# Layers, merge outputs and MLP down tiles: the high weights times both token halves as one 512-column matmul, and the two sums added at eviction

## The reference, cut to what matters

```
# first block, twice
h = rms_norm(x, norm_g);  p = h @ w_in                # fox, diff, moba: q, k, v, gate; gla: q, k, v, gate; a few small columns
fox  = forgetting_attention(q, k, v, log_f) * silu(gate)
diff = rms_norm((softmax(q1 k1) - lam * softmax(q2 k2)) v) * (1 - lambda_init) * silu(gate)   # q, k rotated
moba = moba_attention(rotated q, rotated k, v) * silu(gate)                                  # one block of 256: causal
gla  = rms_norm(gla_chunked(q, k, v, log_a)) * silu(gate)
x = x + concat(fox, diff, moba, gla) @ w_out
# second block, once
p, pc = modulate(norm(x)) @ in_w, modulate(norm(ctx)) @ in_w[:, :A_COLS + B_COLS]
ya, yb = rwkv7_branch(...), gdn_branch(...)           # recurrences over the context, then over the tokens, in both directions
x = x + g1 * ((gate_a * (ya @ up_a) + gate_b * (yb @ up_b)) @ out_w)
x = x + g2 * (square(relu(modulate(norm(x)) @ mlp_w1)) @ mlp_w2)
out = rms_norm(x)
```

## Time and profile before

| | |
|---|---|
| median of three runs | 3850.47 us (3849.56, 3850.47, 3851.57) |
| profiled execution | 3848.72 us, span 3846.6 us |
| mean granted clock of TensorE | 0.984 |
| busy, share of the span | PE 96%, PEld 89%, DVE 54%, POOL 43%, ACT 39% |
| DMA | 153 GB/s in the mean |

### The profile page before, as it was taken

The page is one execution under the profiler, slowest core; times in us unless marked ns, Lnnn a source line. Parts: engine busy times, 40 slices in busy tenths (PEclk is TensorE's granted clock), DMA queues, the critical chain, the costliest instruction groups (busy, mean ns, idle before and its releaser), DMA issues. The chain is left out here.

```text
span 3846.6 us, 85962 instructions
## 1 busy us (share of the span) xinstructions
PE 3682.1 (96%) x37216; PEld 3409.0 (89%) x37216; DVE 2084.0 (54%) x3808; ACT 1504.8 (39%) x2641; POOL 1659.3 (43%) x1195
## 2 busy tenths in 40 slices
PE   7999999999998999999899999999988999999998
PEld 7999898999986888888688888888888999999998
DVE  5545425444336776677766666666547553435343
ACT  5344434444434432322233333333334453435353
POOL 5555556555544543333311111111115566666664
PEclk9999999999989999999999999999999999999999
DMA  6445454454445777778410000100007445455553
GB/s 238 169 180 181 187 196 156 167 185 176 175 154 175 259 261 266 250 258 293 154 32 20 15 24 28 28 20 15 3 2 263 176 176 187 177 186 184 179 186 131
DMA packets 116391, 587.20 MB, mean 153 GB/s; under 512 B 20912, under 2 KB 40496, under 8 KB 51376
## 3 DMA queue, kind: packets, MB, share of 16 engines
q1 hardware_dynamic: 116016, 581.71, 42.5%
HBM read 560.95 MB, written 20.71 MB: 151 GB/s over the span
## 5 line engine op out<-in xcount | busy, mean ns | idle before, releaser
L557 PE MATMUL bank<-act_L,part_L 128*128 128x256 f32 x7296 | 946.6, 288 | 12.4 <-DMA cst<-in_cst 4.6
L557 PEld LDWEIGHTS bank<-act_L,part_L 128*128 128x128 f32 x7296 | 901.0, 193 | 49.1 <-issue 30.6
L557 PE MATMUL bank<-act_P,part_P 128*128 128x512 f32 (+1 forms) x3488 | 716.1, 365 | 17.9 <-POOL part_P L3013 12.8
L3013 POOL TENSOR_TENSOR part_L<-wring,part_L 128x512 fp32r<-128x512 f32 x304 | 532.8, 1754 | 458.0 <-ACT part_L L1325 449.7
L3013 POOL TENSOR_TENSOR part_C<-wring,part_C 128x512 fp32r<-128x512 f32 x320 | 567.6, 1782 | 370.1 <-ACT part_C L1325 370.1
L557 PEld LDWEIGHTS bank<-act_P,part_P 128*128 128x128 f32 x3488 | 590.4, 188 | 136.9 <-DVE arena_P L2437 16.0
L557 PE MATMUL bank<-arena_B 64*64 64x64 f32 (+2 forms) x11200 | 544.4, 231 | 39.2 <-DVE arena_B L2550 21.0
L557 PEld LDWEIGHTS bank<-arena_B 64*64 64x64 f32 (+2 forms) x11200 | 481.3, 143 | 89.2 <-DVE arena_B L2550 23.4
L3013 POOL TENSOR_TENSOR part_P<-wring,part_P 128x512 fp32r<-128x512 f32 x184 | 306.1, 1669 | 428.1 <-ACT part_P L1325 428.1
L1325 ACT ACTIVATE part_C<-wring 128x1024 fp32r<-128x1024 f32 x320 | 338.4, 1058 | 355.8 <-PE bank L557 352.7
L557 PE MATMUL bank<-act_Y,part_C 128*128 128x258 f32 (+1 forms) x3840 | 463.7, 283 | 9.5 <-POOL part_C L3013 9.5
(11 more groups left out here) (250 smaller groups left out, 3483.0 us busy)
## 6 DMA issues: line engine op xcount, KB each, us to landing
wring<-in_w SPq DMA_DIRECT2D x404, 1024.0 KB, 4.8
arena_P<-in_w SPq DMA_DIRECT2D x64, 1024.0 KB, 5.2
mring<-in_w SPq DMA_DIRECT2D x32, 1024.0 KB, 6.6
z_kept<-arena_P SPq DMA_DIRECT2D x34, 256.0 KB, 5.6
z_kept<-arena_P SPq DMA_DIRECT2D x58, 128.0 KB, 5.4
xT<-z_kept SPq DMA_DIRECT2D x26, 256.0 KB, 2.8
arena_C<-z_kept SPq DMA_DIRECT2D x32, 128.0 KB, 3.4
cst<-z_kept SPq DMA_DIRECT2D x24, 128.0 KB, 2.1
```

Source lines behind the costliest of these rows:

```text
L557: return e.matmul(out, lhsT, rhs, start=start, stop=stop)
L3013: e.tensor_tensor(wl[:, 4:8, :], wring[s % NS][:, 8 * j + 4:8 * j + 8, :], wh[:, 4:8, :].bitcast(F32), sub).then_inc(*mark("pool_lo", "lop ...
```

## The change

1. `project`: where X is 256 tokens wide and the tile isn't one of the merge's `apart`, Wh by Xh and Wh by Xl become one matmul of 512 columns into both halves of the bank, as in P. Wl by Xh goes to the first half as before. `b[:, 0:256]` then holds Wh Xh + Wl Xh, `b[:, 256:512]` holds Wh Xl. This takes in all 76 tiles of both layers, the 16 merge outputs and the 64 MLP down tiles.
2. `rest` (transposes or rotation into the upper half of the bank before) is called after k = 5 and not k = 3.
3. Input tiles: ScalarE copies the upper half, scaled, to where the sum is to be; then VectorE adds the lower half to it, and that releases the bank or `raw`. The gates have four instructions: ScalarE copy, VectorE sum (frees the bank), in the next tile's place for `rest` ScalarE tanh into `L.rope`, VectorE (tanh + 1) times the sum.
4. Output tiles, merge outputs, MLP down: a second VectorE instruction adds the upper half to xT and frees the bank.
5. The small products of the gates at tiles 1 and 2 now stand ahead of those tiles' evictions.

```diff
@@ project (TensorE)
+                    wide = X.shape[-1] == 256 and not apart
...
-                        mm(o, wh[:, k, :], x[:, 0, :], first and k == 0, False)
-                        mm(o, wh[:, k, :], x[:, 1, :], False, False)
+                        if wide:
+                            mm(b.rearrange("p (s t) -> p s t", s=2), wh[:, k, :], x, first and k == 0, False)
+                        else:
+                            mm(o, wh[:, k, :], x[:, 0, :], first and k == 0, False)
+                            mm(o, wh[:, k, :], x[:, 1, :], False, False)
                         t = mm(o, wl[:, k, :], x[:, 0, :], False, end and k == 7)
+                        if k == 5 and j == 0 and rest is not None:
+                            rest()
                         if k == 3:
-                            if j == 0 and rest is not None:
-                                rest()
@@ evac (ScalarE), input tiles
-                        cp(L.raw[n % 3], ps, SCALE.get(kind, 1.0)).then_inc(*mark("act_layer", "raw", l, n))
...
-                        af(L.mix[:, m, :], ps, ACT.Tanh, scale=0.5).then_inc(*mark("act_layer", "gate", l, n))
+                    cp(dst, b[:, 256:512], SCALE.get(kind, 1.0)).then_inc(*mark("act_layer", "low", l, n))
@@ rest (ScalarE), gates
+                        w.wait_ge(done("sum", l, n))
+                        af(L.rope, L.mix[:, gate_of(n), :], ACT.Tanh, scale=0.5).then_inc(*mark("act_layer", "gate", l, n))
@@ evac (VectorE), input tiles
+                    w.wait_ge(done("low", l, n))
+                    if what == "g":
+                        mx = L.mix[:, gate_of(n), :]
+                        tt(mx, b[:, 0:256], mx, add).then_inc(*mark("dve_layer", "free", "pj", u))
...
+                    elif what == "v" or g in ("diff", "moba"):
+                        r = L.raw[n % 3]
+                        stt(r, b[:, 0:256], scale, r, mult, add).then_inc(*mark("dve_layer", "raw", l, n))
+                    else:
...
+                        stt(dst, b[:, 0:256], scale, dst, mult, add).then_inc(*mark("dve_layer", "free", "pj", u))
@@ rest (VectorE), gates
+                        stt(L.mix[:, m, :], L.rope, 1.0, L.mix[:, m, :], add, mult).then_inc(*mark("dve_layer", "gated", l, m))
@@ output tiles, VectorE (merge outputs and MLP down alike, with stt)
-                        tt(xT[:, c, :], xT[:, c, :], b[:, 0:256], add).then_inc(*mark("dve_x", "free", "pj", u))
+                        tt(xT[:, c, :], xT[:, c, :], b[:, 0:256], add).then_inc(*mark("dve_x"))
+                        own("dve_x")
+                        tt(xT[:, c, :], xT[:, c, :], b[:, 256:512], add).then_inc(*mark("dve_x", "free", "pj", u))
```

More of the change, by code:

```diff
@@ L496, in raw_before, with gate_of @@
             return ("rest" if LTILES[m][0][-1] == "v" else "rawfree", l, m)
+        def gate_of(n):
+            kind, h = LTILES[n]
+            return 12 + h if kind == "gg" else 4 * GROUPS.index(kind[:-1]) + h
         def mark(sem, *event):
@@ L1458, in f @@
                         w.wait_ge(done("th", l, 15))
-                        cp(L.raw[n % 3], ps, SCALE.get(kind, 1.0)).then_inc(*mark("act_layer", "raw", l, n))
+                        dst = L.raw[n % 3]
+                    elif g == "g" and what in "qk":
+                        dst = (L.gq if what == "q" else L.gk)[:, h, :]
                     elif what in "qk":
[L1461 to L1467, removed]
-                    else:
-                        m = 12 + h if g == "g" else 4 * GROUPS.index(g) + h
-                        af(L.mix[:, m, :], ps, ACT.Tanh, scale=0.5).then_inc(*mark("act_layer", "gate", l, n))
+                        dst = (L.q if what == "q" else L.k)[i % 2]
+                        w.wait_ge(done("score", l, i - 2, 0)) if i >= 2 else None
+                    else:
+                        dst = L.mix[:, gate_of(n), :]
+                    cp(dst, b[:, 256:512], SCALE.get(kind, 1.0)).then_inc(*mark("act_layer", "low", l, n))
                 return f
@@ L1476, in layer_in @@
                     yield from project("L", 76 * l + n, evac(l, n), beside)
+                    if n == 59:
+                        rest(l, n)()
                     if n == 0:
@@ L2159, in rest, with f @@
                 g, what = kind[:-1], kind[-1]
+                if what == "g":
+                    def f():
+                        m = gate_of(n)
+                        w.wait_ge(done("gate", l, n))
+                        own("dve_layer")
+                        stt(L.mix[:, m, :], L.rope, 1.0, L.mix[:, m, :], add, mult).then_inc(*mark("dve_layer", "gated", l, m))
+                    return f
                 if not (what in "qk" and g in ("diff", "moba")):
@@ L2179, in evac @@
                 g, what = kind[:-1], kind[-1]
-                if what != "g":
-                    return None
-                m = 12 + h if g == "g" else 4 * GROUPS.index(g) + h
+                i = (n - 12) // 4
                 def f(b, u):
[L2185 to L2188, removed]
+                    scale = SCALE.get(kind, 1.0)
+                    w.wait_ge(done("low", l, n))
+                    if what == "g":
+                        mx = L.mix[:, gate_of(n), :]
+                        tt(mx, b[:, 0:256], mx, add).then_inc(*mark("dve_layer", "free", "pj", u))
+                        counts.at[("sum", l, n)] = counts.last("dve_layer")
+                    elif what == "v" or g in ("diff", "moba"):
+                        r = L.raw[n % 3]
+                        stt(r, b[:, 0:256], scale, r, mult, add).then_inc(*mark("dve_layer", "raw", l, n))
+                    else:
+                        if g == "g":
+                            dst, name = (L.gq if what == "q" else L.gk)[:, h, :], (kind, l, h)
+                        else:
+                            dst, name = (L.q if what == "q" else L.k)[i % 2], (what, l, i)
+                        stt(dst, b[:, 0:256], scale, dst, mult, add).then_inc(*mark("dve_layer", "free", "pj", u))
+                        counts.at[name] = counts.last("dve_layer")
                 return f
@@ L2193, in layer_in, with ev @@
                 for n in range(60):
-                    ev = {1: lambda b, u: gates_in(l, at), 2: lambda b, u: gates_out(l)}.get(n, evac(l, n))
+                    def ev(b, u, n=n):
+                        if n == 1:
+                            gates_in(l, at)
+                        elif n == 2:
+                            gates_out(l)
+                        evac(l, n)(b, u)
                     yield from project("L", 76 * l + n, ev, rest(l, n - 1) if n else None)
+                    if n == 59:
+                        rest(l, n)()
                     if n == 0:
@@ L2916, in ev @@
                         w.wait_ge(done("g1h"))
-                        stt(xT[:, c, :], b[:, 0:256], K.g1h[:, c:c + 1], xT[:, c, :], mult, add).then_inc(*mark("dve_x", "free", "pj", u))
+                        stt(xT[:, c, :], b[:, 0:256], K.g1h[:, c:c + 1], xT[:, c, :], mult, add).then_inc(*mark("dve_x"))
+                        own("dve_x")
+                        stt(xT[:, c, :], b[:, 256:512], K.g1h[:, c:c + 1], xT[:, c, :], mult, add).then_inc(*mark("dve_x", "free", "pj", u))
                         counts.at[("x", 3, c)] = counts.last("dve_x")
@@ L2974, in ev @@
                         own("dve_x")
-                        stt(xT[:, c, :], b[:, 0:256], mod[:, 80 + c, 0:1], xT[:, c, :], mult, add).then_inc(*mark("dve_x", "free", "pj", u))
+                        stt(xT[:, c, :], b[:, 0:256], mod[:, 80 + c, 0:1], xT[:, c, :], mult, add).then_inc(*mark("dve_x"))
+                        own("dve_x")
+                        stt(xT[:, c, :], b[:, 256:512], mod[:, 80 + c, 0:1], xT[:, c, :], mult, add).then_inc(*mark("dve_x", "free", "pj", u))
                         counts.at[("x", 4, c)] = counts.last("dve_x")
```

5 lines of the change are left out of this document (4 added, 1 removed).

## The result

The changed kernel takes 3832.63 us in the median of five runs (3830.91 to 3834.19), the kernel before 3851.20 beside it. The ratio is 0.995, with a 95% interval of 0.9939 to 0.9961: 18.6 us faster, or 15 to 23 by the interval. The prediction was 3820 in a range of 3802 to 3838. The time is in the range and the direction is right, but the gain is 60% of the 30.7 us forecast, and the time lies 1.6 us above the likeliest case's own range (3806 to 3831). What was mis-sized is the subject of the rest.

A forecast was written before the change was run, and what follows sets the result against it. TensorE's queue was taken as the bound, plus short waits in the layers. Terms: -37.8 + 1.5 + 1.7 + 0.9 + 3 = -30.7 us, from 3848.72 to 3818.0; with medians 1.75 higher, 3820 us, range 3802 to 3838.

The forecast's parts named there:

- likeliest case: The forecast itself for the whole kernel: gain 20 to 45 us, own range 3806 to 3831, chance 0.69.
- the gain's mechanism: TensorE, wide tiles: each matmul costs 0.013 us over its columns, whichever its width; 3712 matmuls go.
- overhead goes with columns: Rival on TensorE's matmuls: 512-column step 0.240 us, pair 0.360, no gain, 7 us of waits stay; 3857, chance 0.05.
- VectorE's queue: Rival: VectorE stops at all 120 input tiles until ScalarE has copied, delaying queued work; 37 us slower, 3888, chance 0.05.
- The signs: Timeline checks: merge and MLP 9 to 17 us shorter, layers 10 to 27; layers far under twice the rest means waits.
- The pace: Wide tiles on TensorE: a 512- plus 256-column pair takes 0.3466 or 0.353 us, not 0.360; middle gain 37.8 us.
- The two bounds: TensorE's gain from the removed matmuls: 49.7 us at 0.3466 us a pair, 26.0 us at 0.353.
- Item 3: Start of the GLA part in each layer: tile 4's sum is queued ahead on busy VectorE; 0.9 us charged.
- Item 2: Last head of each layer: copy, sum, tanh and product now come before the mask; 1.7 us charged.
- Item 1: Ends of both layers and the MLP: one more add before the square that TensorE waits for; 1.5 us charged.
- Item 4: Some 20 places where TensorE already waits for fixed chains: faster tiles find them later; 3 us, bounds 0 and 8.
- What hides the rest: Added evictions at merge outputs, MLP down, layer outputs, steady input tiles and gates: covered by slack, cost 0.

The follow-up runs named there:

- e9_queue: Changed kernel with only tile 4's sum moved ahead of four GLA instructions in VectorE's queue: 3823.61 us, against 3831.68 for the changed kernel run again.
- e4_rest3: Changed kernel with rest (transposes and rotation) called after k = 3 of the first half and not k = 5: 3838.82 us.
- e5_tiles4_59: Changed kernel with tiles 4 and 59 of each layer (first value tile, last gate) narrow and evicted as before: 3825.00 us, against 3853.21 before the change.
- e12_best: Changed kernel with tile 4's sum earlier in VectorE's queue, odd k's matmuls turned (also P's 256-token tiles), tile 59 narrow: 3816.62 us.
- e1_halves: Changed kernel with the 512-column matmul taken apart into two of 256, new evictions kept: 3865.05 us, against 3850.79 before the change.
- e3_order: Changed kernel with the two matmuls of every odd k swapped in wide tiles: 3825.33 us, 7.3 less than the changed kernel.
- e7_rest7: Changed kernel with rest (transposes and rotation) called after k = 7 of the first half and not k = 5: 3834.99 us.
- e11_queue_order: Changed kernel with tile 4's sum earlier in VectorE's queue and odd k's matmuls turned in wide tiles and P's 256-token tiles: 3816.97 us.

## Why the prediction was right in its sign and short in its size

- **What bounds it, and the gain's mechanism: right.** TensorE's queue is the bound, a step costs 0.013 us over its columns, and 3712 matmuls fewer gave time. The rivals "overhead goes with columns" and "VectorE's queue" over the whole of the layers fell. The signs came out as put: 10.1 us less in the layers and 8.8 in merge outputs and MLP, far from twice as much, so waits took part of the gain.
- **The pace: the mechanism right, the size off.** 37.8 us was the middle of 26.0 and 49.7; 32.4 was measured by the medians, 30.2 by the stretches that the edit touches. The merge outputs and the MLP are nearly all slow (8.8 us, by 80 x 16 pairs x 0.007 = 9.0), the layers mixed (21.4). The two bounds held. That the middle is near is luck: it was a choice for want of a reason, and what picks the pace isn't known now either. The range's lower end, 3802, is below what its own terms give (3850.5 - 49.7 + 4 = 3804.8). The guess that the contiguous X might help was wrong where it could be seen alone, in the MLP.
- **Item 3, the GLA starts: the step that failed most.** I put 0.9 us, with "the sum of tile 4 is queued ahead". It is queued behind the GLA work: 69.46 and not 65.0. The half tiles around it (the two of tile 5 and the first of tile 6) are 4.1 and 3.9 us longer than before in the two layers, and e9_queue gave 8.1 back. The earlier trace rows showed a busy VectorE from 64.17 on; what I didn't do was to place the new instruction in the program's order among those rows. The rival on VectorE's queue was the same mechanism, spread over the input tiles where at k = 5 it acts in the first value tile of each layer, and at k = 3 in a few heads as well (e4_rest3).
- **Item 2, the last heads: right.** Mask 458.84 - 456.93 = 1.91 us after ScalarE's copy, 1.8 foretold, 0.95 before; the waits are 8.7 us against 6.8, 1.9 more and 1.7 foretold, and 6.8 again with tile 59 narrow (e5_tiles4_59, e12_best).
- **Item 1, the three ends: right as far as seen.** e1_halves has the half tiles after the first layer's end 0.7 us longer than before, where 0.5 was charged.
- **Item 4, existing short waits, 3 us: the size about right, the reason in part wrong.** The sixteen half tiles of the heads in which the changed kernel didn't get faster with the others, or got slower, come to 2.7 us. But in e1_halves, where no tile runs faster, the heads are 1.2 us longer than before all the same (0.5 and 0.7 in the table), in half tiles that are mostly the same ones. So nearly half of it belongs to the evictions and the place of rest, and not to tiles that run faster.
- **What hides the rest: nearly right.** Merge outputs, MLP and layer outputs: no cost seen. Input tiles at k = 5: the 1.2 us just named, besides the GLA starts. Among TensorE's listed waits in the layers none is for a DMA, before or after.
- **The sum, again with what was measured:** -32.4 + 14.3 = -18.1 against the forecast -30.7. Both terms are differences to e1_halves, so their sum proves nothing; the parts are what tells. The evictions (items 1 to 3) were put at 4.1 us. They cost 11.3 in the layers: 7.8 in the half tiles of the GLA starts where 0.9 was put, and 3.5 elsewhere where items 1 and 2 had 3.2. The matmuls, less item 4, were put at 34.8 and gave 32.4. So of the 12.6 us that are missing 6.9 are the GLA starts and 2.4 the pace with item 4; 3.0 are the P and recurrences of e1_halves's trace, and their part in the medians isn't known.

The Trainium skill's 2.5 ns over the columns for an isolated matmul (TensorE: Matmul & The Clock Gate, Part 2, Back-to-back issue gap) would have given 9 us for the matmuls alone, an estimate. e1_halves gives 32.4 for 3712 of them, 8.7 ns each: the runs don't agree with 2.5 ns in this stream, where each matmul has its own weight load.

## What to carry to other kernels

When a change puts a new short instruction on an engine that isn't the bound, ask not how busy that engine is but which instructions stand ahead of it at each place, above all where a burst of other work begins; one such place in each layer cost 4 us, and all the other input tiles together less than that. Split a change into its two halves by experiment (here: new evictions, old matmuls) before judging either. And read the pace of a stream as start-to-start over many steps: the same two widths ran at 0.3467, 0.348 or 0.353 us a pair, 0.348 with the order turned; which of the other two a stretch falls into isn't explained here.

## What the hardware showed that I had not expected

- **Two self-keeping paces of one stream.** 512- and 256-column matmuls in strict turn take 0.3467 or 0.353 us a pair. In the slow pace the starts follow each other in a pattern of three pairs (0.233 + 0.117, 0.241 + 0.120, 0.236 + 0.113 us in the MLP), in the fast one of two (0.233 + 0.117, 0.231 + 0.112). All of a quarter's 256 pairs stayed slow; turning every second pair gives 0.348 in all 160 half tiles of merge outputs and MLP (e3_order).
- **Short falls of TensorE's clock in a full queue.** The kernel before has one half tile of 4.37 us late in the second layer, with no wait in it; the window (length, busy PE, clock, DMA share, GB/s) shows why:

```profile
1101.00:1104.00 3.00, 3.00 (x27) 1.00 0.32 49
1104.00:1108.00 4.00, 4.00 (x23) 0.57 0.55 229
```

  The granted clock fell to its lower level (1.2 GHz) for most of the second window, with TensorE busy throughout on either side, and a 256-column step took 0.213 us there. It cost 1.5 us, and such half tiles stand at other places in other traces. In P, past its first 20 us, four of the fourteen traces have one such fall (e1_halves, e5_tiles4_59, e7_rest7, e11_queue_order), and P is 1.5 to 1.7 us longer in them than in the trace of the nearest kernel without it.
- **The recurrences vary by 5 us between the traces** (1092.0 to 1097.5), though no edit touches them, and by 2.6 us between two traces of one program; that is more than several of the effects here. In the traces of 1095 us and more the granted clock stood at its lower level for 82 to 92 us of that stretch (e12_best: 92), in the others for 72 to 82; that the one is the cause of the other isn't shown. Differences under 3 us can be read only stretch by stretch.
